# Meta keys' share of the attention outputs as one fp32r product over 48 stacked rows

## The reference, cut to what matters

```python
def block(qblk):                                   # 128 queries of one head
    s = jnp.einsum('bqhcd,bkhcd->bhcqk', qblk, kh) * scale
    p = jax.nn.softmax(s, axis=-1)                 # over all 528 keys
    p_diff = p[:, :, 0] - lam * p[:, :, 1]
    return jnp.einsum('bhqk,bkhv->bqhv', p_diff, vh)
```

## Time and profile before

| | |
|---|---|
| median of 3 runs | 1386.17 us (1385.78 to 1386.58) |
| the profiled execution's own time | 1386.22 us |
| its span | 1384.4 us |
| granted TensorE clock | 0.999 |
| busy: PE / PEld / DVE / ACT / POOL | 1369.9 / 1291.0 / 1046.2 / 837.3 / 186.0 us |
| chain that ended last | PE 89%, DVE 5%, ACT 2%, issue 2% |

### The profile page before, as it was taken

One profiled execution on the slowest core, in us unless ns is written; L12 is line 12 of the kernel. 1 busy time (PEld: TensorE's weight loads), 2 busy tenths in 40 slices (PEclk: granted clock), 3 DMA queues, 4 the chain that ended last, 5 costly groups with the idle time before them and its releaser, 6 DMA issues.

```text
span 1384.4 us, 32303 instructions
## 1 busy us (share of the span) xinstructions
PE 1369.9 (99%) x13108; PEld 1291.0 (93%) x13108; DVE 1046.2 (76%) x1765; ACT 837.3 (60%) x1802; POOL 186.0 (13%) x158
## 2 busy tenths in 40 slices
PE   9999999999999999999999999999999999999998
PEld 9999999998999999999998888888888899999987
DVE  6888887788646777877667888888886478888864
ACT  7666666666434666666555667666664456666654
POOL 1111222220000000000001122222210000000100
PEclk9999999999999999999999999999999999999999
DMA  5332322332323333333233232333323233334432
GB/s 188 117 98 93 108 85 86 108 108 78 99 71 122 101 99 100 103 90 100 70 107 108 87 106 85 108 107 108 108 82 108 85 110 107 108 107 114 114 96 76
DMA packets 76340, 140.41 MB, mean 101 GB/s; under 512 B 9504, under 2 KB 39456, under 8 KB 76192
## 3 DMA queue, kind: packets, MB, share of 16 engines
q1 hardware_dynamic: 76192, 138.35, 33.0%
HBM read 112.36 MB, written 17.30 MB: 94 GB/s over the span
## 4 chain that ended last, share of the span: by engine, by line
PE 89%; DVE 5%; ACT 2%; issue 2%; DMA 0%; SPq 0%; DVEq 0%; ACTq 0%
PE proj L1926 64%; PE far L2191 5%; PE pair L2174 3%; PE pair L2176 3%; PE far L2208 2%; PE pair L2059 1%; PE far L2193 1%; PE far L2144 1%; PE far L2145 1%; PE pair L2124 1%; DVE ops L1660 1%; PE pair L1926 1%; PE pair L2131 1%; DVE w_lo L1392 1%; PE far L2148 1%
## 5 line engine op out<-in xcount | busy, mean ns | idle before, releaser
L1926 PE MATMUL proj<-u_hi,w_hi 128*128 128x264 f32 (+1 forms) x1960 | 478.7, 312 | 1.9 <-DVE w_lo L1392 0.7
L1926 PE MATMUL proj<-u_lo,w_hi 128*128 128x264 f32 (+1 forms) x1960 | 458.2, 302 | 0.0
L1926 PE MATMUL proj<-u_hi,w_lo 128*128 128x264 f32 (+1 forms) x1960 | 458.1, 302 | 0.0
L1926 PEld LDWEIGHTS proj<-u_hi,w_hi 128*128 128x128 f32 x1960 | 314.7, 189 | 19.3 <-issue 1.4
L1926 PEld LDWEIGHTS proj<-u_hi,w_lo 128*128 128x128 f32 x1960 | 314.0, 188 | 13.6
L1926 PEld LDWEIGHTS proj<-u_lo,w_hi 128*128 128x128 f32 x1960 | 314.0, 188 | 10.6
L1392 DVE TENSOR_TENSOR w_lo<-w_raw,w_hi 128x1024 fp32r<-128x1024 f32 x178 | 221.9, 1247 | 35.9 <-ACT w_hi L952 35.8
L1200 ACT ACTIVATE decay<-pair,neg_max 128x528 f32<-128x528 f32 (+1 forms) x144 | 100.3, 697 | 203.4 <-DVE neg_max L1782 203.3
L952 ACT ACTIVATE w_hi<-w_raw 128x1024 fp32r<-128x1024 f32 x178 | 186.5, 1048 | 39.4 <-PE proj L1926 36.6
L1782 DVE TENSOR_REDUCE neg_max<-pair 128x1 f32<-128x528 f32 (+1 forms) x144 | 101.4, 704 | 90.5 <-PE pair L2176 89.3
L892 POOL TENSOR_TENSOR mix_lo<-mixed_t,mix_hi 128x528 fp32r<-128x528 f32 (+1 forms) x32 | 50.9, 1590 | 502.0 <-ACT mix_hi L1247 502.0
(11 more groups left out here) (257 smaller groups left out, 2245.7 us busy)
## 6 DMA issues: line engine op xcount, KB each, us to landing
w_raw<-w_units SPq DMA_DIRECT2D x178, 512.0 KB, 3.6
v_scratch<-blocks SPq DMA_DIRECT2D x128, 64.0 KB, 2.1
v_rows<-v_scratch SPq DMA_DIRECT2D x32, 256.0 KB, 2.9
o_scratch<-blocks SPq DMA_DIRECT2D x104, 64.0 KB, 2.7
q_stack<-gate_f SPq DMA_DIRECT2D x32, 132.0 KB, 2.4
k_stack<-k_stack SPq DMA_DIRECT2D x32, 132.0 KB, 2.4
o_rows<-o_scratch SPq DMA_DIRECT2D x14, 256.0 KB, 3.8
ops<-o_scratch SPq DMA_DIRECT2D x12, 256.0 KB, 2.6
```

Of the source, the lines that this page charges most:

```text
L1926: ins = pe.matmul(out, w, x[:, tile, cols_n], start=(k == 0 and p == 0), stop=(k == last_k and p == 2))
```

## The change

The meta keys' product becomes one fp32r product. A number in fp32 is written as a rounded fp32r part and the rest, x = x_hi + x_lo. With p_hi, p_lo, p_hi on 48 rows of `p_stack`, and v_hi, v_hi, v_lo on the same rows of `v_stack`, one product gives p_hi v_hi + p_lo v_hi + p_hi v_lo. The rows from 48 up are zeroed once. The parts are made before the transposes, with queries (for p) or value columns (for v) still on the 128 partitions and 16 keys along the row; one transpose of 48 columns in the place of one of 16 then puts them on the rows.

```diff
+META_PARTS = 3
+META_ROWS = META_PARTS * N_META
# POOL, setup
+            pool.memset(v_stack[:, :].bitcast(f32), 0.0).then_inc(pads_set, 1)
+            pool.memset(p_stack[:, :].bitcast(f32), 0.0).then_inc(pads_set, 1)
# POOL, new; called as split_values(l, c + 1) for the attention heads, between cut_mixed(n - 1) and invert_rms(n)
+            def split_values(l, c):
+                t, a = l * LAYER_UNITS + value_unit(c), l * AT_HEADS + c - HG_HEADS
+                pool.wait_ge(evacuated[t % 2], evac_count(t))
+                if a > 0:
+                    pool.wait_ge(v_turned, l * HEADS + c - (HG_HEADS if c == HG_HEADS else 0))
+                meta_values = v_t[:, 0:N_META]
+                pool.tensor_copy(v_parts[:, 0, 0:N_META], meta_values).then_inc(v_rounded, 1)
+                pool.tensor_copy(v_parts[:, 1, 0:N_META], meta_values).then_inc(v_rounded, 1)
+                pool.wait_ge(v_rounded, 2 * (a + 1))
+                pool.tensor_tensor(v_parts[:, 2, 0:N_META], meta_values, v_parts[:, 0, 0:N_META].bitcast(f32),
+                                   ALU.subtract).then_inc(v_split, 1)
# ACT, copy_v for the attention heads, and copy_turned
+                    act.activation(v_stack[0:META_ROWS, :], meta[0:META_ROWS, 0:P], ACT.Copy).then_inc(v_ready, 1)
-                act.activation(cols[0:N_META, 4, 0:rows], meta[0:N_META, 0:rows], ACT.Copy)\
+                act.activation(p_stack[0:META_ROWS, 0:rows], meta[0:META_ROWS, 0:rows], ACT.Copy)\
# DVE, new; called right behind the p row of every query chunk
+            def split_probs(j, r, chunks_before):
+                at = chunks_before + j
+                dve.wait_ge(p_ready, at + 1)
+                p = qk_dec[r, j % 2, 0, 0:N_META]
+                dve.tensor_copy(p_parts[r, j % 2, 0:3:2, 0:N_META], p.unsqueeze(1).to_broadcast([r.stop, 2, N_META]))\
+                    .then_inc(p_rounded, 1)
+                dve.wait_ge(p_rounded, at + 1)
+                dve.tensor_tensor(p_parts[r, j % 2, 1, 0:N_META], p, p_parts[r, j % 2, 0, 0:N_META].bitcast(f32),
+                                  ALU.subtract).then_inc(p_split, 1)
# PE, turn_v, for c >= HG_HEADS
+                    pe.wait_ge(v_split, l * AT_HEADS + c - HG_HEADS + 1)
+                    pe.transpose(meta[0:META_ROWS, 0:P], v_parts[:, :, :].rearrange("p b r -> p (b r)").bitcast(f32),
+                                 ident[:, :]).then_inc(v_turned, 1)
# PE, attend
-                    pe.matmul(meta[:, 0:P], cols[:, 4, :], v_meta[:, :],
+                    pe.matmul(meta[:, 0:P], p_stack[:, :], v_stack[:, :],
                               start=False, stop=True).then_inc(pv_done, 1)
-                    pe.transpose(meta[0:N_META, 0:rows], p[:, 0:N_META], ident[0:rows, 0:rows])\
-                        .then_inc(p_turned, 1)
+                    pe.wait_ge(p_split, chunks_before + j + 1)
+                    pe.transpose(meta[0:META_ROWS, 0:rows],
+                                 p_parts[0:rows, j % 2, :, :].rearrange("p b r -> p (b r)").bitcast(f32),
+                                 ident[0:rows, 0:rows]).then_inc(p_turned, 1)
```

More of the change, by code:

```diff
@@ L452, in encoder_trunk @@
         v_meta = sb("v_meta", [P, P])
+        v_parts = sb("v_parts", [P, META_PARTS, N_META], f32r)
+        v_stack = sb("v_stack", [P, P], f32r)
+        p_parts = sb("p_parts", [P, 2, META_PARTS, N_META], f32r)
+        p_stack = sb("p_stack", [P, P], f32r)
         cols = sb("cols", [P, 2 * N_CHUNKS, P])
@@ L513, in encoder_trunk @@
         v_ready = sem("v_ready")
+        v_rounded = sem("v_rounded")
+        v_split = sem("v_split")
+        p_rounded = sem("p_rounded")
+        p_split = sem("p_split")
         k_turned = sem("k_turned")
@@ L933, in _ @@
                         cut_mixed(n - 1)
+                    if HG_HEADS <= c + 1 < HEADS:
+                        split_values(l, c + 1)
                     invert_rms(n)
@@ L1066, in copy_v @@
                 act.wait_ge(v_turned, n + 1)
+                if n % HEADS >= HG_HEADS:
+                    act.activation(v_stack[0:META_ROWS, :], meta[0:META_ROWS, 0:P], ACT.Copy).then_inc(v_ready, 1)
+                    return
                 act.activation(v_meta[0:N_META, :], meta[0:N_META, 0:P], ACT.Copy).then_inc(v_ready, 1)
@@ L1249, in _ @@
             act.wait_ge(ones_set, 4)
-            act.wait_ge(pads_set, 6)
+            act.wait_ge(pads_set, 8)
             load_root_table()
@@ L1815, in attend @@
                                              ALU.mult, ALU.add).then_inc(p_ready, 1)
+                    split_probs(j, r, chunks_before)
             dve.wait_ge(gain_in, 16)
@@ L2026, in turn_v @@
                     pe.wait_ge(o_taken, l * HEADS + c)
+                if c >= HG_HEADS:
+                    pe.wait_ge(v_split, l * AT_HEADS + c - HG_HEADS + 1)
+                    pe.transpose(meta[0:META_ROWS, 0:P], v_parts[:, :, :].rearrange("p b r -> p (b r)").bitcast(f32),
+                                 ident[:, :]).then_inc(v_turned, 1)
+                    return
                 pe.transpose(meta[0:N_META, 0:P], v_t[:, 0:N_META], ident[:, :]).then_inc(v_turned, 1)
```

## The result

The changed kernel takes 1388.45 us (median of 22 runs, 1387.32 to 1389.91) against 1386.26 us (22 runs) before: a ratio of 1.0016, interval 1.0009 to 1.0022, 2.2 us more. The forecast was 1387.9. The profiled execution took 1388.21 us.

A forecast was written before the change was run, and what follows sets the result against it. PE was taken to bound the kernel (busy 99%, 89% of the last chain), with new DVE waits eating its 8.0 us: -0.15 - 0.03 + 7 x 0.09 + 7 x 0.18 = +1.7 on 1386.22, so 1387.9, range 1382.5 to 1391.0.

The forecast's parts named there:

- PE's gain: Meta product on PE: one fp32r record for two fp32 ones saves 0.111 us, times 72, 8.0 us if kept.
- The rival with fp32r at fp32's price: Meta product: fp32r at 128 columns takes as long as fp32, so slower, about 1389.6 us; chance 0.17.
- DVE's pair: Two small DVE instructions behind each of 72 p rows: 0.41 us a pair, bounds 0.30 and 0.50, 29.5 us in all.
- Place 1: Query chunk 2's transposes: chunk 1's pair delays DVE, PE comes early, cover is 0.12; PE waits 0.3 to 0.5 us.
- Place 2: Next head's first score, through late q_stack and k_stack DMAs: layer 0 heads at most 0.17 us longer, taken as 0.09.
- Layer 1, the step that failed: Layer 1's next first score: heads at most 0.36 us longer, taken as 0.18; the fifth transpose's wait costs nothing.
- c = 8: Heads c = 8, once a layer: the pair's 0.41 us shows in full; with PE's gain, -0.15 and -0.03 us.

The follow-up runs named there:

- e1: The changed kernel without DVE's two split instructions per query chunk, the parts of p staying zero: 1379.73 us.
- s1: The changed kernel with DVE's pair left out for query chunk 1 of every head alone: 1384.48 us.
- b6: The kernel before with only two moves: DVE's gates product behind chunk 2's p, POOL's mix_lo in layer 1 held until the next head's low queries are cut: 1386.18 us.
- e3: The changed kernel with DVE's copy alone, without the subtraction, so p_lo stays zero: 1382.55 us.
- e4: The changed kernel with POOL's mix_lo of layer 1's heads 9 to 14 held until query chunk 3's split is made: 1386.16 us.
- k1: The changed kernel with p's parts made by POOL instead of DVE, and the 48-column transpose behind its step's first projection piece: 1382.15 us.
- k2: k1 with the 48-column transpose put right behind the other four for query chunks 1 and 4: 1383.50 us.
- k3: k2 with DVE's product with the gates moved behind query chunk 2's p in heads 9 to 14: 1383.80 us.

## Why the prediction was right, and where it was not

- **PE's gain**, 0.111 us a product, 8.0 in all: right, 0.112 by the loads; e1 keeps 6.5 us of it and loses 1.2 at chunk 2. The rival with fp32r at fp32's price fell.
- **DVE's pair**, 0.41 us: right, 0.42 by the starts (0.18 and 0.17 us, each 0.03 us behind its predecessor). The statement of the Trainium skill that was weighed ("VectorE: DVE Perf Modes", The DRAIN you can't avoid), that the semaphore between DVE instructions costs nothing extra, does not fit here either: the subtraction starts 0.22 us behind the cast that it depends on, and w_lo, which depends on neither, 0.09 behind the subtraction.
- **Place 1**, 0.3 to 0.5 us at chunk 2's transposes: right in the number, 0.41 to 0.45, and s1 shows the cause that was named. The sum behind the number had two errors that nearly cancel, and that is luck. The 0.12 us between p and PE's load was taken for cover. But in the changed kernel and in e1, where PE does wait, the load starts 0.12 us behind p too. In the trace before, the load stands 0.18 us behind the one ahead of it; in b6, where p ends 0.6 us earlier, 0.14. So in layer 0 PE already waited some 0.04 us there (in layer 1, at 0.15 behind p, it had 0.03 to spare). The room was on DVE, as idle time without a bracket between chunk 1's w_lo and the next row maximum, which needs PE's scores. PEld before and in b6, then DVE before and after:

```profile
488.17 0.19 PEld L2176 LDWEIGHTS pair<-k_low,q_stack 128*128 128x128 f32 x1
...
488.09 0.19 PEld L2180 LDWEIGHTS pair<-k_low,q_stack 128*128 128x128 f32 x1
488.23 0.47 PEld L2212 LDWEIGHTS far<-ident,qk_dec 128*128 128x128 f32 x4
...
480.31 0.77 DVE L1814 SCALAR_TENSOR_TENSOR qk_dec<-decay,row_inv 128x528 f32<-128x528 f32 x1
481.00 1.22 DVE L1392 TENSOR_TENSOR w_lo<-w_raw,w_hi 128x1024 fp32r<-128x1024 f32 x1
482.31 0.71 DVE L1782 TENSOR_REDUCE neg_max<-pair 128x1 f32<-128x528 f32 x1
...
482.42 0.70 DVE L1823 TENSOR_REDUCE neg_max<-pair 128x1 f32<-128x528 f32 x1
```

From p to that row maximum it is 2.00 us before, 2.03 in e3 with the cast alone and 2.25 in the changed kernel (480.17 to 482.42): of the pair's 0.42 us, 0.17 vanish there, and 0.25 arrive at chunk 2's p. With the 0.2 us that PE comes early they make the 0.45. It is 12 heads and not 14: in c = 15 the gates' product stands at step 2, so that the stretch on DVE has room; I had taken the heads as alike.
- **Place 2**, the next head's first score: in layer 0 right in kind: PE loses 0.09 to 0.13 us there, 0.34 at head 10. The q_stack DMAs leave at 500.29 against 499.54 before, while the head's stretch on DVE started 0.14 us earlier (479.10 for 479.24): 0.89 us late, where the sum had 1.06. The difference is the same 0.17 us of idle time without a bracket. Heads 9 to 15 of layer 0 together came out 0.3 us shorter, not 0.6 longer.
- **Layer 1, the step that failed.** The prediction let the fifth transpose's wait cost nothing and put 0.18 us a head at the first score. The first score is in time there; the fifth transpose waits 0.43 us, since POOL's mix_lo holds up the cast. A head is 0.34 us longer, twice the forecast; heads 9 to 15 together 1.75 us and not 1.3. The trace before showed it: a rotary step of 1.80 us among others of 0.70, in just the place where the pair was to go. I priced the pair by rows without a neighbour on POOL. "SBUF — State Buffer" of the Trainium skill (Who interferes with whom) states that DVE and GpSimd share a pair of SBUF ports: a DVE cast that runs in a two-port mode contends for it, and so does a DVE instruction with two SBUF inputs beside a GpSimd one that reads SBUF; the lock is exclusive, and who issues first decides who blocks. The rows above agree, in both directions (1.14 us for 0.18 on DVE, 1.13 for 0.20 on POOL, each ending within 0.05 us of the other engine's instruction), and in e4, where mix_lo starts behind the cast, the cast takes 0.18.
- **c = 8**: +0.28 and not +0.41. The cast takes the wait behind POOL (1.19 us) that the gates took before (1.84 us, now 0.70), so that only part of the pair is added:

```profile
363.52 1.19 DVE L1814 CAST p_parts<-qk_dec 128x32 fp32r<-128x32 f32 x1
364.75 0.18 DVE L1817 TENSOR_TENSOR p_parts<-qk_dec,p_parts 128x16 fp32r<-128x16 f32 x1
364.84 0.70 DVE L1573 SCALAR_TENSOR_TENSOR gates<-stage 128x528 f32<-128x528 f32 x1
```

The sum came within 0.6 us of the median, in part by errors of opposite sign: layer 0 was forecast 0.9 us too dear, layer 1 0.5 too cheap, and in this pair of profiles 0.3 us more come from the HGRN heads of layer 1 and 0.5 from behind PE's last weight load, which no experiment here was made to explain. What held is the main reason: the waits on a DVE without room eat the 8 us of PE time.

## What to carry to other kernels

Where PE's wait ends just in time, time won on PE is worth nothing until the producer has room too: count the cover at each meeting point, in each kind of head, and set against it what PE will have won by then. A small gap behind the producer need not be cover: look at a place where the consumer does wait, and see how far behind it starts there (0.12 us here). A small instruction costs its place, not its length: look in the trace before for instructions at that place that take longer than their kind, and ask who will wait for the new one. If another engine is idle most of the time, give it the work and put its reader behind other work, as k1 does; but check what runs beside it.

## What the runs showed of the hardware

- A cast of 32 elements a partition takes 0.18 us alone and 1.1 to 1.2 us behind a POOL instruction with SBUF inputs; a POOL cast takes 0.20 us alone and 1.13 behind a DVE subtraction of 1.22 us. The mean over 64 casts of the changed kernel is 0.303 us, 0.212 in e4: a mean well over the usual duration is the sign of it.
- An fp32r product of 128 columns with a full weight load takes 0.11 us, and a transpose of 48 columns no more from PE than one of 16.
- A load of weights on 16 partitions starts 0.33 us behind a load on 128 partitions, whether its data came 1.1 or 5.9 us earlier, and 0.06 behind another on 16; loads on 128 follow each other at 0.11 to 0.12.
- SP issues two q_stack or k_stack DMAs in 1.1 to 1.25 us, but in single heads it takes longer: 1.79 once in the trace before, and 1.69 to 2.52 ahead of layer 0's c = 14 in e3, e4, k1, k2 and k3. The next first score then waits 0.36 to 0.88 us by the weight loads. Two profiles can differ by this alone, which is why sums over heads were read and not one span.
